# A hybrid decoder layer in float32: the second feed-forward matmul as seven block products per pair of slabs

## The reference

```python
mod = silu(c) @ w_ada + b_ada            # six vectors of 2048: shift, scale, gate for each sub-layer
h = modulate(rms_norm(x, g_pre_mix), sh1, sc1)
...                                      # input projection, RG-LRU group, attention group
y = concat([rms_norm(y_lru), rms_norm(y_att)]) @ w_out
x = x + gt1 * rms_norm(y, g_post_mix)
h = modulate(rms_norm(x, g_pre_mlp), sh2, sc2)
y = square(relu(h @ w_ff1)) @ w_ff2      # 2048 -> 8192 -> 2048
x = x + gt2 * rms_norm(y, g_post_mlp)
```

## Time and profile before

| | |
|---|---|
| median of 3 runs | 2311.75 us (2310.22 to 2312.07) |
| profiled execution, span | 2307.4 us |
| last matmul ends, last output operation ends | 2298.9, 2304.2 us |
| chunk of 1024 in the loop | 179.55 us |
| PE, DVE, ACT, POOL busy | 96%, 50%, 29%, 6% |
| transfers | 321.49 MB, 139 GB/s over the span |

### The profile page before, as it was taken

One profiled execution on the slowest core, in us unless ns is written; L12 is line 12 of the kernel. 1 busy time (PEld: TensorE's weight loads), 2 busy tenths in 40 slices (PEclk: granted clock), 3 DMA queues, 4 the chain that ended last, 5 costly groups with the idle time before them and its releaser, 6 DMA issues.

```text
span 2307.4 us, 24341 instructions
## 1 busy us (share of the span) xinstructions
PE 2207.3 (96%) x9441; PEld 1762.1 (76%) x9441; DVE 1163.0 (50%) x1410; ACT 666.6 (29%) x897; POOL 149.0 (6%) x134
## 2 busy tenths in 40 slices
PE   4779999999889989999999999999999999999998
PEld 3557778888667778778888888888888888888886
DVE  7998695456884657843332332422332342333335
ACT  4224622222553253222222312311221221221232
POOL 3451040000120000000000000000000000000000
PEclk7889999999999999999999999999999999999999
DMA  9874456637425645842333223233223223323342
GB/s 332 287 231 152 141 188 195 189 116 261 132 87 183 219 144 179 274 133 83 106 95 91 92 92 98 82 105 95 91 92 98 92 91 94 97 91 92 99 165 91
DMA packets 178308, 321.49 MB, mean 139 GB/s; under 512 B 12184, under 2 KB 47112, under 8 KB 176192
## 3 DMA queue, kind: packets, MB, share of 16 engines
q1 hardware_dynamic: 172576, 303.12, 41.3%
q0 software_dynamic: 3408, 16.92, 2.2%
q10 hardware_dynamic: 2256, 0.53, 0.1%
HBM read 312.13 MB, written 8.40 MB: 139 GB/s over the span
## 4 chain that ended last, share of the span: by engine, by line
PE 84%; DVE 11%; ACT 3%; issue 2%; DMA 1%; DVEq 0%; ACTq 0%
PE bank L356 14%; PE bank L357 14%; PE bank L358 14%; PE bank L368 13%; PE bank L367 13%; PE bank L366 13%; DVE acc L1068 6%; DVE LP L1203 1%; DVE stat L1198 1%; DVE w_lo L1039 0%; DVE yg L1313 0%; PE bank L530 0%; DVE LP L1195 0%; ACT w_hi L712 0%; ACT junk L941 0%
## 5 line engine op out<-in xcount | busy, mean ns | idle before, releaser
L1331 DVE TENSOR_TENSOR w_lo<-raw,w_hi 128x1024 fp32r<-128x1024 f32 x253 | 308.3, 1223 | 704.2 <-ACT w_hi L986 703.8
L356 PE MATMUL bank<-h_hi,w_lo 128*128 128x512 f32 x1536 | 620.0, 404 | 17.1 <-POOL h_lo L1457 10.8
L357 PE MATMUL bank<-h_lo,w_hi 128*128 128x512 f32 x1536 | 614.7, 400 | 0.0
L358 PE MATMUL bank<-h_hi,w_hi 128*128 128x512 f32 x1536 | 614.2, 400 | 0.0
L986 ACT ACTIVATE w_hi<-raw 128x1024 fp32r<-128x1024 f32 x253 | 267.0, 1059 | 980.4 <-PE bank L368 487.0
L368 PE MATMUL bank<-w_hi,u_hi 128*128 128x512 f32 x1024 | 408.4, 399 | 0.0
L367 PE MATMUL bank<-w_lo,u_hi 128*128 128x512 f32 x1024 | 403.5, 394 | 0.0
L366 PE MATMUL bank<-w_hi,u_lo 128*128 128x512 f32 x1024 | 402.9, 393 | 0.0
L356 PEld LDWEIGHTS bank<-h_hi,w_lo 128*128 128x128 f32 x1536 | 293.6, 191 | 93.7 <-issue 17.7
L357 PEld LDWEIGHTS bank<-h_lo,w_hi 128*128 128x128 f32 x1536 | 293.4, 191 | 71.6 <-issue 1.4
L358 PEld LDWEIGHTS bank<-h_hi,w_hi 128*128 128x128 f32 x1536 | 293.0, 191 | 71.9
(11 more groups left out here) (215 smaller groups left out, 1638.8 us busy)
## 6 DMA issues: line engine op xcount, KB each, us to landing
raw<-in_w_ff_dram SPq DMA_DIRECT2D x256, 512.0 KB, 3.7
raw<-in_w_ada_dram SPq DMA_DIRECT2D x128, 512.0 KB, 4.6
raw<-in_w_in_dram SPq DMA_DIRECT2D x82, 512.0 KB, 3.9
gst<-in_w_ada_dram SPq DMA_DIRECT2D x64, 512.0 KB, 6.0
raw<-in_w_out_dram SPq DMA_DIRECT2D x32, 512.0 KB, 4.5
x_tok<-in_x_dram SPq DMA_DIRECT2D x4, 1024.0 KB, 8.3
xr<-in_x_dram POOLq DMA_DIRECT2D x4, 1024.0 KB, 7.0
x_scratch<-yg POOLq DMA_DIRECT2D x4, 1024.0 KB, 4.7
```

The source lines that it names most:

```text
L356: pe.matmul(b[:, :], lo[:, cols], act_hi[:, kt, :], start=(kt == 0), stop=False)
L357: pe.matmul(b[:, :], hi[:, cols], act_lo[:, kt, :], start=False, stop=False)
L358: last = pe.matmul(b[:, :], hi[:, cols], act_hi[:, kt, :], start=False, stop=(kt == n_kt - 1))
L1331: dve.tensor_tensor(w_lo[:, s], raw[:, slot], w_hi[:, s].bitcast(F32), ALU.subtract).then_inc(lo_ready, 1)
```

## The change

The second product is done by Winograd's form of Strassen's scheme. A chunk has 512 hidden columns (16 chunks). Its activations are cut into 2 x 2 blocks (two halves of the hidden columns, two halves of the tokens), `w_ff2` of the chunk likewise (two halves of the rows, two sides of the 2048 columns). Each side is taken in two slabs of 512 columns (r = 0, 1). For each r seven block products replace eight, so a chunk has 14 products of 12 matmuls. The last chunk is multiplied in the plain way, as eight units.

- Weights: a `w_ff2` unit (256 rows x 512 columns) is loaded into a raw slot of its own; DVE makes four sums per r (`w2_total`), ACT and DVE split seven operands per r (`w2_high`, `w2_low`) into two buffers.
- Activations: seven operands of 2 x 256 columns, three of them by way of sums (`operand_total`), are split once per chunk (`operand_high`, `operand_low`).
- PSUM is four pairs of banks. The first product of the next chunk uses pairs 0 and 1 and the block products pairs 2 and 3. DVE adds each product into one or two blocks of `y2` (`read_product`, 16 operations of 1024 columns a chunk); `y2` is zeroed by POOL first.
- `w_ff1` comes as slabs of two k tiles in two buffers of their own (`w1_raw`). Two pieces (one slab, 24 matmuls) stand ahead of each product in `W_BEFORE`.
- ACT's part of the next chunk's operands is `next_operands`; DVE's list for a chunk is `iteration` below.
- Conditioning units: two behind each of the 16 weight units in the out-projection, the last 16 in chunk 0; gates 4 to 7 go through a scratch row in DRAM.

```diff
-    CHUNKS = 8
+    CHUNKS = 16
-        return (U_ATT + 2 <= n < U_OUT + 2) + (U_OUT + 3 <= n < U_OUT + 19) + 2 * (U_MLP + 8 <= n < U_MLP + 24)
+        return (U_ATT + 2 <= n < U_OUT + 2) + 2 * (U_OUT + 3 <= n < U_OUT + 19)
+    W_BEFORE = [2, 0, 2, 0, 2, 0, 2, 0, 2, 0, 2, 2, 2, 0]
+    W_MADE = {1: 2, 3: 3, 5: 4, 7: 5, 9: 6, 10: 7, 11: 8, 13: 9}
...
+            sp.wait_ge(y_sum, 4)
+            for j in range(8):
+                if j >= 2:
+                    sp.wait_ge(w1_lo, j - 1)
+                load_w1((0, 0), j)
+                for pos in (POS_MLP + 2 * j, POS_MLP + 2 * j + 1):
+                    load(pos)
...
-                    pe.wait_ge(gate_ready, r - 1)
+                if r:
+                    pe.wait_ge(gate_ready, r)
-                        if v == (0, 2, None, 2, 2)[r]:
+                        if v == (0, 2, 1, 1, 2)[r]:
...
+            def product(ck, n, first=False):
+                r, i = divmod(n, 7)
+                pe.wait_ge(w2_lo, of(ck, PRODUCTS, n + 1))
+                if r == 0:
+                    pe.wait_ge(op_lo_ready, of(ck, 7, i + 1))
+                if n:
+                    before = 8 * ((n - 1) // 7) + READS_BEFORE[(n - 1) % 7]
+                    if before or not first:
+                        pe.wait_ge(product_read, of(ck, 16, before))
...
+            for q in range(HALVES):
+                pe.wait_ge(h2_lo_ready, q + 1)
+                w1_piece((0, 0), q)
+                if q == 11:
+                    pe.wait_ge(x1t_copied, 4 * NT)
+                    row_job(22, pairs[2][:, 0, :])
+            row_job(23, pairs[3][:, 0, :])
+            pe.wait_ge(gate_ready, 8)
...
+            def w1_high(ck, j, first=False):
+                act.wait_ge(w1_in[j % 2], of(ck, 64, 16 * (j // 2 + 1)))
...
+                    act.wait_ge(w1_used, of(ck, 8, j - 1))
+                act.activation(w_hi[:, 2 + j % 2], w1_raw[:, j % 2], ACT.Copy).then_inc(w1_hi, 1)
...
+            def next_operands(ck, first=False):
+                rectify(ck, 0, first)
+                rectify(ck, 1, first)
+                square_u(ck, 0)
+                w2_high(ck, 0, first)
+                operand_high(ck, A11, first)
+                square_u(ck, 1)
...
-                for q, at in ((1, 7), (2, 15), (3, 19)):
+                for q, at in ((1, 7), (2, 10), (3, 15), (4, 19)):
...
+            def iteration(ck, first=False, last=False):
+                for n in range(PRODUCTS):
+                    if n < 6:
+                        operand_low((ck, 0), n + 1)
+                    if n < 3:
+                        operand_total((ck, 0), n + 2)
+                    if n == PRODUCTS - 1 and not last:
+                        operand_low((ck, 1), A11)
+                        operand_total((ck, 1), S_1)
+                    read_product((ck, 0), n, first)
+                    if n < PRODUCTS - 2:
+                        w2_low((ck, 0), n + 2)
...
+                    if n + 3 < PRODUCTS:
+                        if (n + 3) % 7 in SUM_OF:
+                            w2_total((ck, 0), n + 3)
...
+                    if n in W_MADE and not (last and W_MADE[n] >= 8):
+                        w1_low((ck, 1), W_MADE[n])
...
             for kt in range(KT):
                 modulate(kt)
                 if kt >= 3 and kt % 2:
-                    lo_of_chunk(0, LAG + (kt - 3) // 2)
-                    for a in ada_of[U_MLP + LAG + (kt - 3) // 2]:
-                        ada_unit(a)
+                    w1_low((0, 0), (kt - 3) // 2 + 2)
+                    for a in (0, 1):
+                        ada_unit(ADA_MLP + kt - 3 + a)
+                if kt == 13:
+                    take_gate(6, pairs[2][:, 0, :])
+            for a in (N_ADA - 2, N_ADA - 1):
+                ada_unit(a)
+            take_gate(7, pairs[3][:, 0, :])
```

More of the change, by code:

```diff
@@ L328, in _ @@
-            with sp.Fori(1, CHUNKS - 1) as ck:
-                chunk(ck)
-            chunk(CHUNKS - 1)
+            sp.wait_ge(y_sum, 4)
[5 more added lines that the diff above has]
+                    load(pos)
+            for j in range(2):
+                sp.wait_ge(w1_lo, 7 + j)
+                load_w1((1, 0), j)
+            for which in range(4):
+                sp.wait_ge(ada_used, N_ADA - (len(stream) - 1 - which) % RING)
+                load_w2((0, 0), 0, which)
@@ new lines, in product @@
+            def product(ck, n, first=False):
[7 more added lines that the diff above has]
+                        pe.wait_ge(product_read, of(ck, 16, before))
+                elif not first:
+                    pe.wait_ge(product_read, of(ck, 16, -1))
+                bank = pairs[2 + (i + r) % 2]
+                fresh = i in (0, 1, 5, 6)
+                for k in range(2):
+                    hi, lo = w_tile(n % 2, k)
+                    for tt in range(2):
+                        tok = slice(tt * P, (tt + 1) * P)
+                        pe.matmul(bank[:, tt, :], op_lo[:, i, k, tok], hi, start=(fresh and k == 0), stop=False, skip_group_check=True)
+                        pe.matmul(bank[:, tt, :], op_hi[:, i, k, tok], lo, start=False, stop=False, skip_group_check=True)
+                        last = pe.matmul(bank[:, tt, :], op_hi[:, i, k, tok], hi, start=False, stop=(k == 1), skip_group_check=True)
+                last.then_inc(product_done, 1)
@@ new lines, in _, with last_unit @@
+            row_job(23, pairs[3][:, 0, :])
+            pe.wait_ge(gate_ready, 8)
+            iteration(0, first=True)
+            with pe.Fori(1, CHUNKS - 2) as ck:
+                iteration(ck)
+            iteration(CHUNKS - 2)
+            def last_unit(e, tiles=range(NT)):
+                half = e % 2
+                for k in range(2):
+                    hi, lo = w_tile((2, 3, 0, 1)[e % 4], k)
+                    for t in tiles:
+                        bank = pairs[e // 2 % 2 * 2 + t // 2][:, t % 2, :]
+                        i, tok = ((A11, A12), (S_1, A22))[t // 2][half], slice(t % 2 * P, (t % 2 + 1) * P)
+                        pe.matmul(bank, op_lo[:, i, k, tok], hi, start=(half == 0 and k == 0), stop=False)
+                        pe.matmul(bank, op_hi[:, i, k, tok], lo, start=False, stop=False)
+                        done = pe.matmul(bank, op_hi[:, i, k, tok], hi, start=False, stop=(half == 1 and k == 1))
+                return done
@@ L1527, in _ @@
             load_x(1)
[L1528 removed]
+            for q in (3, 4, 5):
                 load_gain(q)
+            store_gate2(4)
             for t in range(NT):
```

596 lines of the change are left out of this document (389 added, 207 removed).

## The result

The kernel with the change takes 2318.24 us (median of 7 runs, 2315.55 to 2320.71) beside 2311.11 us for the kernel before on the same chip (7 runs, 2308.76 to 2312.07): ratio 1.0031, 95% interval [1.0021, 1.0041]. It is 0.3% slower. 2302 us and "faster" were forecast. The profiled execution has a span of 2318.4 us, where the earlier trace rows has 2307.4 and the prediction's sum gave 2297.9: 20.5 us are missing. Of these some 4 are a difference between executions. In every run of the kernel after, its own time is 1.8 us above its span; so the 4.35 that the prediction adds to get from the span of before to a median are 1.8 and, by estimate, 2.5 by which that profiled execution was faster than the median. The profiled execution of after (2320.21 us) is 2.0 above its median. Between medians 2318.24 - 2302 = 16.2 us are missing.

The account below looks back on a forecast made before the run. Bound by the number of matmuls. -84.2 + 7.6 + 6.0 + 33.2 + 5.3 + 2.7 + 4.1 + 9.8 + 6.0 = -9.5 us: span 2307.4 to 2297.9, plus 4.35 gives 2302 us; range 2282 to 2320.

Parts of the forecast that it names:

- a gain of 84: Second product: 360 matmuls fewer at 0.2338 us each, -84.2 us.
- "Out-projection", +7.6 and +6.0 and 4.0 of clock: Out-projection: TensorE waits for gate 1 before group 2 and gate 3 before group 4; slow starts 2.0 us each.
- +4 if transfers come late as well: Out-projection: upper bound stated beside the two gate waits, +4 us, for late transfers.
- closed loop of load and use in chunk 0: Chunk 0: from slab 4, each slab issued only after conditioning units behind the previous low part; period 10.5 us.
- "First matmul of chunk 0", +33.2: Chunk 0 head: slabs held by conditioning units, loop entered 79.9 us after the first matmul, +33.2 us.
- in chunk 0 the slowed slabs still fit the 10.5: Chunk 0: slabs with matmuls at the slow clock still fit the 10.5 us slab period, adding nothing.
- Loop, +5.3 and +2.7: Loop: product 3 is 0.38 us late in 14 iterations, +5.3; products 1 and 3 in chunk 0, +2.7.
- last chunk, +4.1: Before the last chunk: four operands are made after the last product is read, +4.1 us.
- tail, +9.8: Last token tiles: DVE's chain of 5.26 us a tile sets the pace instead of matmuls, +9.8 us.
- A: Rival: loop becomes bound by the DVE and ACT path; 1.2 us more per chunk give 2319 us; chance 0.25.
- B: Rival: slabs of chunk 0 are not held up by the conditioning units, 2269 us; chance 0.08.
- C: Rival: the out-projection keeps its pace, 2284 us; chance 0.12.

Follow-up runs that it names:

- early row products, the gain and the spreading: Kernel after with row products behind each group's first weight unit, gate 3's gain requested earlier, out-projection conditioning units over 21 weight units: ratio 0.9940 to kernel before.
- small sums: Kernel after with the 32 out-projection conditioning units multiplied and added on 64 of 512 columns only, transfers and order kept: ratio 1.0002 to the kernel before.
- the added operations: Kernel after with two useless 512-column DVE operations added in each of 15 loop iterations: ratio 1.0111 to the kernel before, +18.5 us against the kernel after.
- the slabs ahead: Kernel after with SyncE issuing each w_ff1 slab of chunk 0 ahead of conditioning units formerly before it: ratio 0.9917 to the kernel before, -26.3 us against the kernel after.

## Why the prediction was wrong

The loop was right to 0.02 us a chunk. The sign turned on the stages around it: a gain of 84 was set against losses of 75, and the losses were some 16 to 20 larger. Three steps failed: the sum for the out-projection (24.6 us for 17.6), the zeroing of y2, which has no term (5.2), and the landing of a slab in chunk 0 (5.9 for 4.6, the largest part of 41.5 for 33.2).

- **"Out-projection", +7.6 and +6.0 and 4.0 of clock: mis-sized.** The stage takes 24.6 us more, not 17.6; waits of 18.4 for 13.6, slow starts of 4.8 for 4.0, and a row product that had no term. The waits at the two gates came as named. What was wrong is DVE's list: 6.5 us of waits were counted from gate 1 to gate 3, and there were 13.3, and "+4 if transfers come late as well" was kept out of the sum. The transfers were late: in the 13 us in which DVE stood, SyncE issued nothing but two conditioning units. The prediction had seen the closed loop of load and use in chunk 0, and did not look for the same loop in the out-projection, where the same two conditioning units share the ring. The runs show that early row products, the gain and the spreading give 21.0 back, and small sums 6.7 only; how much of it is the ring alone is open.
- **The zeroing of y2: left out.** The change says "y2 is zeroed by POOL first"; the sum has no term for it, nor a reason for none. It cost 5.2 us (5.71 - 0.55), and the run without it has them back. POOL is busy for 7% of the span: the share tells nothing of this.
- **"First matmul of chunk 0", +33.2: right mechanism, mis-sized.** Measured +41.5. Six periods of 11.36 for 10.5 make 5.2 of the 8.3: the third of three transfers issued together lands after 5.9 us, not 4.6. The estimate that the prediction worked out from the Trainium skill ("DMA: Bandwidth & Descriptors", section "Anatomy of one DMA — SWDGE (gpsimd) path"), 5.6 for the last of three, was nearer than my choice between the rows 5.1 and 3.7; with six landings it would have made 6 us more in the sum, not the 5 that stand there. That these figures hold for transfers by SyncE in general is not shown: for one alone they make 3.2, and the page of the profile has medians of 3.8 and 4.5 for the two kinds of feed-forward transfers. The rest lies before the first period: "in chunk 0 the slowed slabs still fit the 10.5" was not so for slab 0, since its first 13 matmuls come 0.43 us apart, and the high part of slab 2 waits for the last of its 24 (895.86 for some 893).
- **Loop, +5.3 and +2.7; last chunk, +4.1; tail, +9.8: right.** Product 3 was 0.4 late (0.38 forecast): 84.62 - 360 x 0.2338 = 0.45 a chunk, of which the view calls only 0.15 or nothing a wait. The last wait was 3.74. In the tail DVE paces a tile with 2299.62 - 2294.43 = 5.19 us (5.26 in the earlier trace rows).
- **Rivals.** A needed 1.2 us more a chunk and did not come; the added operations show that it was just that far off. B is false as the kernel stands; with the slabs ahead its mechanism is there, and 26 of its 33 us. C is false: DVE stood 13 us at the buffer, and SyncE with it. What was missing is the rival that came true: losses of the same sign in each of three stages. The chance of "slower" was tied to the loop, the best known part.

## What to carry to other kernels

When work is moved into a stage that shares a ring of buffers, count for each slot who must free it and in which order loads are issued, before adding up busy times: with 62 us of DVE's work and a DMA share of 0.76 to 0.77 in 80 us either way, the placement of the same units, row products and gain decided whether TensorE was busy for 80 or 62 of them. Compare such stretches by the work they hold, not by their busy times alone. Give every added instruction a line in the sum, also one on an idle engine, and look for what runs beside it. Where one large gain is set against many losses, give a chance to several of them being larger at once.

## What the hardware showed that was not expected

- One DVE operation of 128x512 with one SBUF input took 5.71 us beside a GpSimd memset of 6.92 us, and 0.55 with the memset elsewhere; operations with two inputs from SBUF kept their 1.23 and 0.78 us beside a memset of that size.
- In chunk 0 SyncE issued three transfers of 512 KB together, with a pause behind: the two of conditioning units landed after 3.9 us, the slab, issued third, after 5.9 (medians).
- After a wait of 8.8 us TensorE's matmuls run at the 1.2 GHz level (granted clock 0.50 from 754.3 to 759.7, 1.00 from 760), as in the earlier trace rows after 4.3 us: the pieces of matmuls behind 754.31 are 0.43 us long until 759.77, not 0.233, which costs 2.65 us on top of the wait. After 4.99 us, at 913.43, only eight matmuls are slow.
